# Two compressed blocks from three products, with differences of segments and of weights taken on GpSimd

## What is computed

```python
def compress_rows(x, pe, w1, b1, w2):
    b, t, g, dh = x.shape
    nseg = t // CMP_STRIDE                      # 16 rows: 256 segments
    nc = nseg - CMP_SPAN + 1                    # 255 blocks of two segments
    segs = x[:, :nseg * CMP_STRIDE].reshape(b, nseg, CMP_STRIDE, g, dh)
    blocks = jnp.concatenate([segs[:, j:j + nc] for j in range(CMP_SPAN)], axis=2)
    blocks = blocks + pe[:, None, :].astype(x.dtype)
    flat = jnp.moveaxis(blocks, 3, 2).reshape(b, nc, g, CMP_BLOCK * dh)
    return jax.nn.gelu(flat @ w1 + b1) @ w2
```

## Time and profile before

| | us |
|---|---|
| median of 3 runs | 1770.2 (1769.72 to 1770.25) |
| the profiled execution | 1774.92 |
| its span in the trace | 1773.3 |
| TensorE busy | 1677.0 (95%) |
| VectorE busy | 774.6 (44%) |
| ScalarE busy | 321.3 (18%) |
| GpSimd busy | 187.1 (11%) |

### The profile page before, as it was taken

How to read it: one execution, slowest core, us unless ns; L and a number is a source line. 1 busy time by engine, 2 the same in 40 slices (tenths; PEclk the granted TensorE clock), 3 DMA queues, 4 the chain that set the end, 5 groups by cost and what they waited for, 6 DMA issues and landing times. The chain is left out here.

```text
span 1773.3 us, 27018 instructions
## 1 busy us (share of the span) xinstructions
PE 1677.0 (95%) x10248; PEld 1330.4 (75%) x10248; DVE 774.6 (44%) x1758; ACT 321.3 (18%) x814; POOL 187.1 (11%) x329
## 2 busy tenths in 40 slices
PE   8999999999989999999967887889998999999997
PEld 3786989999968777777734555658887888888885
DVE  3442344444334655555740230004567666542334
ACT  2220144343320222222411132100010000000000
POOL 0000100000000000100035665520000000000000
PEclk9999999999989999999978999999999999999999
DMA  8997333333349999732169999876421222222221
GB/s 310 356 330 267 112 98 94 102 98 118 97 156 361 330 363 318 260 114 74 58 225 330 301 350 344 264 262 224 131 76 50 93 71 96 72 95 72 92 75 51
DMA packets 152899, 323.10 MB, mean 182 GB/s; under 512 B 18689, under 2 KB 87618, under 8 KB 152258
## 3 DMA queue, kind: packets, MB, share of 16 engines
q1 hardware_dynamic: 121058, 178.87, 30.7%
q0 software_dynamic: 27104, 129.65, 20.9%
q10 hardware_dynamic: 4608, 12.85, 2.1%
HBM read 303.89 MB, written 109.25 MB: 233 GB/s over the span
## 5 line engine op out<-in xcount | busy, mean ns | idle before, releaser
L974 PE MATMUL bank<-wring,w 128*128 128x128 f32 x2048 | 246.8, 277 | 0.0
L974 PEld LDWEIGHTS bank<-wring,w 128*128 128x128 f32 x2048 | 236.3, 192 | 10.2 <-issue 9.7
L1507 PE MATMUL bank<-hT,wring 128*128 128x272 f32 x704 | 182.4, 398 | 1.2 <-PEq L1234 1.2
L2005 POOL DMA_DIRECT2D ring<-in_sel_pages x256 | 142.6, 557 | 253.2 <-issue 200.7
L1507 PEld LDWEIGHTS bank<-hT,wring 128*128 128x128 f32 x704 | 129.7, 192 | 32.3 <-issue 9.3
L2390 PEld LDWEIGHTS bank<-hT,xk 128*128 128x128 f32 x512 | 99.5, 200 | 51.3 <-issue 30.7
L2390 PE MATMUL bank<-hT,xk 128*128 128x272 f32 x512 | 133.0, 415 | 0.0
L2643 PE MATMUL bank<-hT,wring 128*128 128x272 f32 x392 | 95.4, 392 | 0.0
L2643 PEld LDWEIGHTS bank<-hT,wring 128*128 128x128 f32 x392 | 74.5, 190 | 15.4
L2643 PE MATMUL bank<-aT,wring 128*128 128x272 f32 x352 | 85.9, 392 | 0.0
L322 POOL DMA_DIRECT2D out_new_dil<-in_cache_dil x24 | 16.3, 683 | 626.6 <-POOLq L1234 334.1
(11 more groups left out here) (381 smaller groups left out, 2551.6 us busy)
## 6 DMA issues: line engine op xcount, KB each, us to landing
wring<-in_w SPq DMA_DIRECT2D x147, 512.0 KB, 4.5
out_new_dil<-in_cache_dil POOLq DMA_DIRECT2D x8, 8176.0 KB, 47.4
wring<-in_cmp_pages SPq DMA_DIRECT2D x256, 128.0 KB, 2.1
ring<-in_sel_pages POOLq DMA_DIRECT2D x256, 64.0 KB, 4.7
ring<-in_sel_pages SPq DMA_DIRECT2D x256, 64.0 KB, 4.6
out_new_dil<-in_cache_dil POOLq DMA_DIRECT2D x8, 2032.0 KB, 13.1
ring<-in_dil_k SPq DMA_DIRECT2D x9, 1024.0 KB, 9.3
ring<-in_dil_k POOLq DMA_DIRECT2D x9, 1024.0 KB, 7.9
```

The source lines that it names most:

```text
L974: last = pe.matmul(banks[6 + c % 2][:, P * part:P * part + P].rearrange("p (g a s) -> p g a s", g=G, s=8), w1[:, kv, 8 * hf + jj, :], x[:, ...
L1507: mm = pe.matmul(product_bank(p, n), w[:, P * k:P * k + P], HH[x][:, k, :], start=(k == 0), stop=(k == 3))
L2005: eng.dma_start(slot[:, j, P * i:P * i + P], t["sel_pages"][bass.ds(page, 1), :, P * kv:P * kv + P].rearrange("o p n -> (o p) n")).then_in ...
```

## The change

The cached pages come in a layout that puts keys and values apart and even and odd segments apart; a page is now 2 x 128 x 128. A chunk is 16 pages of keys or of values of one sample (32 chunks as before), and has three parts of 8 matmuls with 128 columns each: the odd segments with W0, the even ones with W1, and the differences of segments, S(2m) - S(2m+1), with the difference of weights, W0 - W1. Block 2m is the sum of the three products; block 2m - 1 is the second of its own m and the first of m - 1. GpSimd takes the differences, one tensor_tensor of 128 x 1024 elements for each chunk and two for the weights. ScalarE writes the first product to two neighbouring columns of `hid` (one instruction for a chunk), VectorE adds the third to the even ones and the second to both (two instructions). The loop's steps 0 to 13 hold 6 parts each, and 12 stand ahead of it; in steps with i = 3 one part instead of two follows the scores.

The loads are one DMA per page for keys or for values in one pair of chunks, and one DMA per page for both in the next pair, into four buffers, one of them the table `row`. The difference buffers lie in a tile of their own and over `cxp`, and those of weights over `qkS` and a part of `con`. So the masks that lay in `con` and `row` are loaded later, in the third stage, ahead of SyncE's loads for product pairs 3 and 18. `hid` has a column more on each side. GpSimd's differences of chunks 0 to 3 stand ahead of its row stores, the others behind them. The same counts of parts are taken in the streams of ScalarE, VectorE and TensorE; only TensorE's are shown for the loop, and the changes of columns from 0 to 1 of `hid` are left out.

```diff
--- before.py
+++ after.py
@@ -197,8 +197,9 @@
     n = len(cmp)
     out = {
-        "cmp_pages": cmp.reshape(n, 8, JJ, 2, 2, G, DH).transpose(0, 3, 6, 4, 5, 2, 1
-                                                                  ).reshape(n, P, 256),
+        "cmp_pages": cmp.reshape(n, 4, 2, JJ, 2, 2, G, DH).transpose(0, 5, 4, 7, 2, 6, 3, 1
+                                                                     ).reshape(n, 2, P, P),
...
         NBLOCKS = 32
-        cxb = [wr[:, 2 * i:2 * i + 2, :].rearrange("p u n -> p (u n)") for i in (1, 2, 0)]
-        s_xl = [sem(f"chunk_landed{i}") for i in range(3)]
+        cx_even = (wr[:, 2:4, :].rearrange("p u n -> p (u n)"), row[:, 0:2 * UNIT])
+        cx_odd = wr[:, :, :].rearrange("p (h u) n -> p h (u n)", h=3)[:, 0::2, :]
+        s_xl = [sem("even_keys_landed"), sem("even_values_landed"), sem("odd_pages_landed")]
...
-        def load_chunk(sp, c):
-            b, q = c // 4, c % 4
-            if c >= 3:
-                sp.wait_ge(s_x, c - 2)
-            for i, page in enumerate(page_numbers(mybir.EngineType.SP, b * PAGES + 8 * q, 8)):
-                sp.dma_start(cxb[c % 3][:, 256 * i:256 * i + 256],
-                             t["cmp_pages"][bass.ds(page, 1), :, :].rearrange("o p n -> (o p) n")
-                             ).then_inc(s_xl[c % 3], 16)
+        def chunk_home(c):
+            return cx_even[c % 2] if c // 2 % 2 == 0 else cx_odd[:, c % 2, :]
+        def chunk_landed(eng, c):
+            eng.wait_ge(s_xl[c % 2 if c // 2 % 2 == 0 else 2], 256 * (c // 4 + 1))
+        def page_of(page, v):
+            return t["cmp_pages"][bass.ds(page, 1), v, :, :].rearrange("o p n -> (o p) n")
+        def load_even(sp, q, v):
+            for i in range(16):
+                if i % 8 == 0:
+                    pages = page_numbers(mybir.EngineType.SP, q // 2 * PAGES + 16 * (q % 2) + i, 8)
+                sp.dma_start(cx_even[v][:, P * i:P * i + P], page_of(pages[i % 8], v)
+                             ).then_inc(s_xl[v], 16)
+        def load_odd(sp, q):
+            for i in range(16):
+                if i % 8 == 0:
+                    pages = page_numbers(mybir.EngineType.SP, q // 2 * PAGES + 16 * (q % 2) + i, 8)
+                sp.dma_start(cx_odd[:, :, P * i:P * i + P],
+                             t["cmp_pages"][bass.ds(pages[i % 8], 1), :, :, :].rearrange(
+                                 "o v p n -> p (o v) n")).then_inc(s_xl[2], 16)
...
-                sp.dma_start(con[:, C_HEAD:], t["con"][:, C_HEAD:]).then_inc(s_sgl, 16)
-                sp.dma_start(row[:, :], t["row"]).then_inc(s_sgl, 16)
+                sp.dma_start(con[:, C_HEAD:C_M4], t["con"][:, C_HEAD:C_M4]).then_inc(s_sgl, 16)
+                sp.dma_start(con[:, C_M1:], t["con"][:, C_M1:]).then_inc(s_sgl, 16)
+                sp.dma_start(row[:, R_SGU:], t["row"][:, R_SGU:]).then_inc(s_sgl, 16)
...
-        hid = sb("hid", [HID, 2, 2, G, NSEG], p2)
-        hsq = sb("hsq", [HID, G, NSEG], p2)
+        hid = sb("hid", [HID, 2, 2, G, NSEG + 2], p2)
+        hsq = att[:, 5376:5376 + G * NSEG].rearrange("p (g s) -> p g s", g=G)
+        cx_diff = (sb("cx_diff", [P, UNIT], p2)[:, :],
+                   cxp[:, :, :, :].rearrange("p v j n -> p (v j n)")[:, 0:UNIT])
+        w_diff = (qkS[:, :, :, :].rearrange("p a b q -> p (a b q)")[:, 0:UNIT], con[:, C_M4:C_M4 + UNIT])
+        s_wd = sem("weights_subtracted")
+        s_xd = sem("segments_subtracted")
...
         class Parts:
             def __init__(self):
-                self.n, self.left = 0, 4 * CHUNKS_FIRST
+                self.n, self.left = 0, 3 * CHUNKS_FIRST
             def step(self):
-                self.left = min(8, 4 * CHUNKS - self.n)
+                self.left = min(6, 3 * CHUNKS - self.n)
...
+        def diff_pool(pool, c):
+            chunk_landed(pool, c)
+            if c >= 2:
+                pool.wait_ge(s_x, c - 1)
+            elif c == 1:
+                pool.wait_ge(s_hid, 2)
+            x = chunk_home(c).rearrange("p (a e n) -> p a e n", a=16, e=2)
+            pool.tensor_tensor(cx_diff[c % 2].rearrange("p (a n) -> p a n", a=16),
+                               x[:, :, 0, :], x[:, :, 1, :], ALU.subtract).then_inc(s_xd, 1)
+        def weights_pool(pool, kv):
+            pool.tensor_tensor(w_diff[kv].rearrange("p (j h) -> p j h", j=JJ),
+                               w1[:, kv, 0:JJ, :], w1[:, kv, JJ:2 * JJ, :],
+                               ALU.subtract).then_inc(s_wd, 1)
         def parts_pe(pe, parts):
             for n in parts:
-                c, part = n // 4, n % 4
-                kv, hf = part // 2, part % 2
+                c, part = n // 3, n % 3
+                kv = c % 2
                 if part == 0:
-                    pe.wait_ge(s_xl[c % 3], 128 * (c // 3 + 1))
+                    chunk_landed(pe, c)
                     if c >= 2:
                         pe.wait_ge(s_xa, c - 1)
-                x = cxb[c % 3].rearrange("p (a v g j s) -> p a v g j s", a=8, v=2, g=G, j=JJ)
+                if part == 2:
+                    if c < 2:
+                        pe.wait_ge(s_wd, kv + 1)
+                    pe.wait_ge(s_xd, c + 1)
+                x = chunk_home(c).rearrange("p (a e g j m) -> p a e g j m", a=16, e=2, g=G, j=JJ)
+                d = cx_diff[c % 2].rearrange("p (a g j m) -> p a g j m", a=16, g=G, j=JJ)
                 for jj in range(JJ):
+                    w, rows = ((w1[:, kv, jj, :], x[:, :, 1, :, jj, :]),
+                               (w1[:, kv, JJ + jj, :], x[:, :, 0, :, jj, :]),
+                               (w_diff[kv][:, P * jj:P * jj + P], d[:, :, :, jj, :]))[part]
                     last = pe.matmul(
                         banks[6 + c % 2][:, P * part:P * part + P].rearrange(
-                            "p (g a s) -> p g a s", g=G, s=8),
-                        w1[:, kv, 8 * hf + jj, :],
-                        x[:, :, kv, :, jj, :].rearrange("p a g s -> p g a s"),
-                        start=(jj == 0), stop=(jj == JJ - 1))
-                if part == 3:
+                            "p (g a m) -> p g a m", g=G, m=4),
+                        w, rows.rearrange("p a g m -> p g a m"), start=(jj == 0), stop=(jj == JJ - 1))
+                if part == 2:
                     last.then_inc(s_x, 1)
+        def chunk_blocks(c, shift):
+            b, h, kv = c // 4, c // 2 % 2, c % 2
+            at = 1 + P * h - shift
+            return hid[:, b % 2, kv, :, at:at + P].rearrange("p g (m e) -> p g m e", e=2)
+        def chunk_product(c, part):
+            return banks[6 + c % 2][:, P * part:P * part + P].rearrange("p (g m) -> p g m", g=G)
+        def both(x):
+            return x.unsqueeze(3).to_broadcast([P, G, 64, 2])
         def parts_act(act, parts):
             for n in parts:
-                c, b, q = n // 4, n // 16, n // 4 % 4
-                if n % 4 < 3:
+                c = n // 3
+                if n % 3 < 2:
                     continue
+                b = c // 4
                 act.wait_ge(s_x, c + 1)
-                if q == 0 and b >= 2:
+                if c % 4 == 0 and b >= 2:
                     act.wait_ge(s_tp, group2_at(2 * b - 3, "project") + 1)
-                for kv in range(2):
-                    last = act.activation(
-                        hid[:, b % 2, kv, :, 64 * q:64 * q + 64],
-                        banks[6 + c % 2][:, 256 * kv:256 * kv + P].rearrange("p (g s) -> p g s", g=G),
-                        ACT.Identity, bias=bias[:, kv:kv + 1])
-                last.then_inc(s_xe, 1)
-
-        def parts_dve(dve, parts):
+                act.activation(chunk_blocks(c, 0), both(chunk_product(c, 0)), ACT.Identity,
+                               bias=bias[:, c % 2:c % 2 + 1]).then_inc(s_xe, 1)
+        def parts_dve(dve, ch, parts):
             for n in parts:
-                c, b, q = n // 4, n // 16, n // 4 % 4
-                if n % 4 < 3:
+                c = n // 3
+                if n % 3 < 2:
                     continue
                 dve.wait_ge(s_xe, c + 1)
-                x = banks[6 + c % 2][:, :].rearrange("p (k f g s) -> p k f g s", k=2, f=2, g=G)[:, :, 1]
-                lo = 1 if q == 0 else 0
-                h = hid[:, b % 2, :, :, 64 * q - 1 + lo:64 * q + 63]
-                dve.tensor_tensor(h, h, x[:, :, :, lo:64], ALU.add).then_inc(s_xa, 1)
+                even = chunk_blocks(c, 0)[:, :, :, 0]
+                ch.link(dve.tensor_tensor(even, even, chunk_product(c, 2), ALU.add))
+                x = chunk_blocks(c, 1)
+                dve.tensor_tensor(x, x, both(chunk_product(c, 1)), ALU.add).then_inc(s_xa, 1)
...
             def _(sp):
-                for c in range(2, CHUNKS):
-                    load_chunk(sp, c)
+                for q in range(1, CHUNKS // 2):
+                    if q % 2:
+                        if q >= 3:
+                            sp.wait_ge(s_x, 2 * q - 2)
+                        load_odd(sp, q)
+                    else:
```

(31 more changed lines are left out.)

34 lines of the change are left out of this document (18 added, 16 removed).

## The result

The changed kernel takes 1749.35 us (median of 4 runs, 1749.16 to 1752.53) against 1770.22 for the kernel before (4 runs, 1769.72 to 1775.52): ratio 0.988, 95% interval 0.986 to 0.989. The forecast of 1727 and its range up to 1742 were too low.

A forecast was written before the change was run, and what follows sets the result against it. TensorE's instruction stream was taken as the bound, everything else hidden beneath it. Parts saved 59 us, less 11 for order and 5 for clock, gave 43: 1770.2 to 1727 us, range 1710 to 1742.

The forecast's parts named there:

- The work that goes: TensorE's page products, 174 to 516 us: a quarter goes, 128 parts becoming 96, saving 59 us.
- Where the gain is given back by the order: ScalarE's chunk copy delays the exponentials, so TensorE waits ahead of four projections; 11.2 us lost with side terms.
- the side term of 0.2 us: Steps between projections: TensorE reaches the first flip nearly level with the norm; 0.2 us taken, 0 to 1.
- The clock: After TensorE's two 3.6 us gaps the clock falls, not after those of 1.9; 2.5 us each, 5 in all.
- rival B: More given back: late differences or loads at head and last steps, clock falls at all four stalls; up to 1741; 18%.
- The GpSimd differences: GpSimd's new subtractions, 2.4 us each, are hidden and TensorE awaits none; 0 us taken, 0 to 5.
- rival C: VectorE and GpSimd obstruct each other; one 2.4 us difference ahead of the chain in 14 steps costs 25 us: 1752; 7%.
- the rule gave about 1 us: VectorE and GpSimd: whole-instruction exclusion for two SBUF inputs, at the assumed starts, would cost about 1 us.
- Loads, masks, small work: SyncE's page loads, moved mask loads and extra VectorE operations stay hidden: 0 us taken, loads 0 to 4.
- The 4.7 us laid to profiling: Whole kernel: the profiled execution's 4.7 us over the median was laid to profiling and carried over, giving 1731.9 profiled.
- The 3.5 us that I took a measurement to resolve: Whole kernel time: a measurement was said to tell 0.2%, 3.5 us, from no change.
- The sum: Whole kernel: 59 - 11 - 5 = 43 us gained, 1727 in plain runs; this forecast had 52%.

The follow-up runs named there:

- late_copy: Changed kernel with ScalarE's chunk copy behind the next pair's exponentials and VectorE's additions behind the norms (three or four key tiles): 1726.5 us, ratio 0.974.
- gaps_filled: Changed kernel with TensorE repeating already computed product parts in the gaps ahead of four projections: 1732.7 us, ratio 0.978.
- no_differences: Changed kernel without GpSimd's 34 subtractions, the third product taking even segments and the first half of the weights: 1734.6 us, ratio 0.980.
- the second set: The changed kernel run once more, unaltered, beside the kernel before: 1739.9 us, ratio 0.982.

## Why the prediction was wrong

**The work that goes: right.** 59 us expected; stage - W - H/2 fell by 58.4. The pace of a part is as before (16 records in 1.95 us).

**Where the gain is given back by the order: right for the step it worked out.** 3.6, 3.6, 1.9 and 1.9 us were expected, 3.54, 3.96, 1.92 and 2.35 measured, and late_copy took away 1.8 of each where there was that much. Too small was the side term of 0.2 us: 1.16 stood ahead of the compressed scores. 12.9 us in all, for 11.2.

**The clock: a term too small.** "So I let the two gaps of 3.6 us lower it and not those of 1.9", 2.5 us each, was drawn from a single gap, the 2.11 us of the earlier trace rows. Measured: 13.7 us in one execution and 10.2 in another, for 5. In the first, 10.2 us stand behind the four gaps that the step had reckoned with, which is what rival B gave them, and 3.4 behind waits for held operations. Two things were wrong: gaps of about 2 us lower the clock more often than not, and the first two had 6.8 us at half clock each in that execution, some 3 us of time (a part lies in the gap), for the 2.5 taken. gaps_filled shows the cause.

**The GpSimd differences: the failed step.** Their length (2.4 us for 2.36) and that TensorE awaits none of them were right. The step went on from there to "all this is hidden ... I take 0". It had asked only who waits for the result, not whom the operation keeps from working. VectorE's operations end with GpSimd's, and 7.2 us of new gaps followed from it (no_differences), with 3.4 us of clock behind them: 10.6 of the 18.6 us that were missing. This was rival C, at 7%, and its mechanism is shown; its reckoning was not. It put one whole difference ahead of the chain in each step, where the holds were on the path at the head, at the first flip and in two steps of the loop. "VectorE then does maxima, or waits for exponentials" was wrong in every kind of step: with four and three key tiles too, small scalings and GELU's products met a subtraction (five of the six-element scalings from 225.30 to 370.13 us took 1.5 to 2.2 us). But there the chain could spare the time, since the four gaps behind it are the same to the hundredth without the subtractions. It could not at the head, at the first flip and with two key tiles, where a load's landing sets GpSimd's start (423.38, behind a DMA).
The Trainium skill's page "SBUF — State Buffer" (section "SBUF: two separate sides") states the rule that the trace bears out: the pair is an exclusive lock for a whole instruction, for a VectorE operation with two SBUF inputs or in its fast mode. The trace agrees for the operations with two inputs in SBUF; the copies and the scaling of 2 to 6 elements have one tensor input there and were held too, maxima were not. In which mode those ran no run shows. At the starts that I had assumed the rule gave about 1 us; the starts were off, not the rule.

**Loads, masks, small work: right at 0.** No gap of TensorE in the stage is put down to a landing, and the later stages kept their length.

**The 4.7 us laid to profiling: wrong.** It did not carry over: the changed kernel's profiled execution took 1749.16 us, its median is 1749.35. The profiled execution of before was one on the slow side of an ordinary spread; in later sets that kernel took 1760 to 1781 us. The 1727 us don't rest on it, being 1770.2 - 43. But it shows in the gain: span against span the change gained 25.8 us, median against median 20.9. The 3.5 us that I took a measurement to resolve were too few as well, for kernels whose executions spread over 10 to 20 us.

**The sum.** Forecast for the stage 59 - 11 - 5 = 43. Measured 58.4 - 12.9 (order) - 7.2 (holds) - 13.7 (clock) = 24.6, against 24.4 by the timeline. In the second set the same kernel's stage gained 30.3 us, the clock giving back 10.2 and the head 2.3 less. The range ended at 1742, just above B's 1741. B had the clock behind the four stalls about right, but no holds and no clock behind them; those were in C, which the range left out with its 1752.

Lengths of the stage rest on one trace each, two for the changed kernel, which differ by 5.8 us. Not settled is what decides whether the 3.05 us gap at 171 us or one of 1.92 us lowers the clock in a given execution. The same streams and the same gap went either way. It was not tried whether a hold could be avoided by other access patterns on VectorE.

## What to carry to other kernels

When a change takes work from the engine that sets the time, recompute for every chain that ended just in time how early the engine now arrives, and price each gap of 2 us and more twice: its length, and half clock behind it. An operation moved to GpSimd is not free when nobody waits for its result: look at what VectorE does in those microseconds, and at whether that chain has cover after the change; here as many subtractions cost nothing that showed in the kernel before and 6 to 12 us of the stage in the changed one. A stage's length less gaps less half of its half-clock time is a quantity that stayed within 3.2 us over the eleven traces with the same products, within 1 us when half clock inside gaps and outside the stage is not counted, and shows what whole times, which spread over 10 us and more, can't.
